# The second feed-forward product with its contraction split over two halves of the array

## The reference, cut to what matters

```
def conv_ffn(h, w_up, conv_w, conv_b, w_down):
    S = h.shape[1]
    u = h @ w_up                                   # 2048 -> 2 * 5632
    up = jnp.pad(u, ((0, 0), (CONV_W - 1, 0), (0, 0)))
    c = conv_b
    for i in range(CONV_W):
        c = c + up[:, i:i + S] * conv_w[i]
    gate, val = jnp.split(c, 2, axis=-1)
    return (jax.nn.gelu(gate, approximate=True) * val) @ w_down   # 5632 -> 2048
...
    x = x + rmsnorm(conv_ffn(h, w_up[l], conv_w[l], conv_b[l], w_down[l]), post_ffn_g[l])
```

## Time and profile before

| | us |
|---|---|
| median of 3 runs | 3087.95 (3086.61 to 3098.1) |
| span of the profiled execution | 3083.6 |
| PE busy in it | 2762.9 (90%) |
| DVE busy | 1585.5 (51%) |
| ACT busy | 1189.2 (39%) |
| first to last matmul start of the job "down" | 1272.5 to 1520.5 |

### The profile page before, as it was taken

The page is one execution under the profiler, slowest core; times in us unless marked ns, Lnnn a source line. Parts: engine busy times, 40 slices in busy tenths (PEclk is TensorE's granted clock), DMA queues, the critical chain, the costliest instruction groups (busy, mean ns, idle before and its releaser), DMA issues.

```text
span 3083.6 us, 33688 instructions
## 1 busy us (share of the span) xinstructions
PE 2762.9 (90%) x13763; PEld 2314.9 (75%) x13763; DVE 1585.5 (51%) x1634; ACT 1189.2 (39%) x1230; POOL 230.3 (7%) x234
## 2 busy tenths in 40 slices
PE   5999999996999999899799978679999598888986
PEld 4876888875887888788688867558888488787875
DVE  3445444644556556544444434565554366655635
ACT  3335333644455445433333454333443222222232
POOL 1002000000000000000000000000000232332210
PEclk9999999998999999999899989889999699989998
DMA  6554666653555555566555533445666401121042
GB/s 187 196 156 48 205 209 203 205 164 132 182 179 175 190 177 177 196 196 194 168 166 191 193 120 110 157 143 177 223 213 205 101 1 29 35 46 34 1 183 90
DMA packets 231320, 459.29 MB, mean 149 GB/s; under 512 B 9767, under 2 KB 29320, under 8 KB 228909
## 3 DMA queue, kind: packets, MB, share of 16 engines
q1 hardware_dynamic: 221584, 419.99, 42.6%
q0 software_dynamic: 8640, 35.36, 4.3%
q10 hardware_dynamic: 988, 2.41, 0.2%
HBM read 443.00 MB, written 14.71 MB: 148 GB/s over the span
## 4 chain that ended last, share of the span: by engine, by line
PE 43%; DVE 5%; ACT 3%; DMA 3%; POOL 3%; SPq 1%; issue 1%; DVEq 0%; ACTq 0%; POOLq 0%
PE bank L286 11%; PE bank L287 11%; PE bank L288 11%; PE bank L1626 2%; DMA d_lora_out<-in_od_a 2%; PE bank L1628 2%; PE bank L1616 2%; PE bank L1461 1%; DMA raw<-in_od_w_o 1%; SPq L1441 1%; PE bank L1584 1%; PE bank L1872 1%; PE bank L386 1%; DVE X L1310 1%; DVE d_step L1643 0%
## 5 line engine op out<-in xcount | busy, mean ns | idle before, releaser
L231 DVE TENSOR_TENSOR w_low<-raw,w_high 128x2048 fp32r<-128x2048 f32 (+1 forms) x384 | 875.8, 2281 | 1087.9 <-ACT w_high L225 1087.8
L225 ACT ACTIVATE w_high<-raw 128x2048 fp32r<-128x2048 f32 (+1 forms) x384 | 732.4, 1908 | 1232.1 <-PE bank L288 1208.3
L286 PE MATMUL bank<-w_high,b_h_high 128*128 128x512 f32 x704 | 278.0, 395 | 12.5 <-DVE w_low L231 10.0
L288 PE MATMUL bank<-w_high,b_h_low 128*128 128x512 f32 x704 | 274.8, 390 | 0.0
L287 PE MATMUL bank<-w_low,b_h_high 128*128 128x512 f32 x704 | 274.5, 390 | 0.0
L286 PE MATMUL bank<-w_high,a_h_high 128*128 128x512 f32 (+1 forms) x640 | 246.4, 385 | 2.1 <-DVE a_bias_rows L735 2.1
L288 PE MATMUL bank<-w_high,a_h_low 128*128 128x512 f32 (+1 forms) x640 | 246.3, 385 | 0.0
L287 PE MATMUL bank<-w_low,a_h_high 128*128 128x512 f32 (+1 forms) x640 | 246.1, 385 | 0.0
L286 PE MATMUL bank<-w_high,d_high 128*128 128x512 f32 x512 | 200.4, 391 | 8.1 <-DVE d_low L1946 8.1
L286 PE MATMUL bank<-w_high,c_x_high 128*128 128x512 f32 x512 | 199.9, 390 | 2.0 <-DVE c_x_low L409 2.0
L287 PE MATMUL bank<-w_low,c_x_high 128*128 128x512 f32 x512 | 199.9, 390 | 0.0
(11 more groups left out here) (365 smaller groups left out, 4548.5 us busy)
## 6 DMA issues: line engine op xcount, KB each, us to landing
raw<-in_w_up SPq DMA_DIRECT2D x88, 1024.0 KB, 5.0
raw<-in_w_in SPq DMA_DIRECT2D x76, 1024.0 KB, 5.1
raw<-in_ev_w_in SPq DMA_DIRECT2D x48, 1024.0 KB, 5.1
raw<-in_w_down SPq DMA_DIRECT2D x44, 1024.0 KB, 5.1
raw<-in_w_out SPq DMA_DIRECT2D x16, 1024.0 KB, 5.2
raw<-in_ev_w_out SPq DMA_DIRECT2D x16, 1024.0 KB, 5.2
raw<-in_od_w_r SPq DMA_DIRECT2D x16, 1024.0 KB, 5.1
raw<-in_od_w_k SPq DMA_DIRECT2D x16, 1024.0 KB, 5.5
```

Of the source, the lines that this page charges most:

```text
L225: act.activation(wh[slot % 2][:, :, 0:width], raw[slot][:, :, 0:width], ACT.Copy).then_inc(sem("w_high_made"), 1)
L231: vec.tensor_tensor(wl[slot % 2][:, :, 0:width], raw[slot][:, :, 0:width], wh[slot % 2][:, :, 0:width].bitcast(F32), ALU.subtract).then_in ...
L286: pe.matmul(b, xh, wh[slot][:, k, 0:width], start=(c == 0 and k == 0), stop=False)
L288: mm = pe.matmul(b, xl, wh[slot][:, k, 0:width], start=False, stop=(c == j.chunks - 1 and k == 3))
```

## The change

Each matmul of the job "down" is replaced by two. One takes rows 0 to 63 of both operands, the other rows 64 to 127; rows of the operands are rows of the array. The first half's sum is kept in bank t (0 or 1), the second half's in bank 2 + t. All four banks now belong to each panel, and at its end ACT copies banks 0 and 1 to `YB`, and DVE adds banks 2 and 3 to it. `acc_free` is incremented by DVE's second addition, and a panel waits for the one just before it (P + 2). The splits of the weights, the transfers and all other jobs are as they were.

```diff
+    def row_products(pe, j, p, g, P, ready=None):
+        width = j.weights(p)[3]
+        pe.wait_ge(sem("acc_free"), P + 2)
+        for c in range(j.chunks):
+            slot = (g + c) % 2
+            hi, lo, k0 = j.stationary(p, c)
+            pe.wait_ge(sem("w_low_made"), g + (c + 1))
+            for k in range(4):
+                if ready is not None:
+                    ready(c, k)
+                first, last = c == 0 and k == 0, c == j.chunks - 1 and k == 3
+                for t in range(2):
+                    for x, w, start, stop in ((hi, wh, first, False), (hi, wl, False, False), (lo, wh, False, last)):
+                        for half in range(2):
+                            r = slice(64 * half, 64 * half + 64)
+                            mm = pe.matmul(PS[2 * half + t][:, 0:width], x[r, k0 + k, 128 * t:128 * t + 128],
+                                           w[slot][r, k, 0:width], start=start, stop=stop)
+            mm.then_inc(sem("w_used"), 1)
+
+    def copy_first_rows(act, j, p, g_end, out):
+        width = j.weights(p)[3]
+        act.wait_ge(sem("w_used"), g_end)
+        act.activation(out(0), PS[0][:, 0:width], ACT.Copy)
+        act.activation(out(1), PS[1][:, 0:width], ACT.Copy).then_inc(sem("first_rows"), 1)
+
+    def add_last_rows(vec, j, p, out):
+        width = j.weights(p)[3]
+        vec.wait_ge(sem("first_rows"), p + 1)
+        vec.tensor_tensor(out(0), PS[2][:, 0:width], out(0), ALU.add)
+        vec.tensor_tensor(out(1), PS[3][:, 0:width], out(1), ALU.add).then_inc(sem("acc_free"), 1)
...
-        run_pe(pe, plan["down"], lambda c, k: pe.wait_ge(sem("ff_low_made"), c + 1) if k == 0 else None)
+        jd = plan["down"]
+        for p in range(jd.panels):
+            row_products(pe, jd, p, jd.g0 + p * jd.chunks, jd.p0 + p,
+                         (lambda c, k: pe.wait_ge(sem("ff_low_made"), c + 1) if k == 0 else None) if p == 0 else None)
...
-        run_act(act, jd, lambda p, t: YB[:, t, PANEL * p:PANEL * p + PANEL])
+        for p in range(jd.panels):
+            for c in range(p * jd.chunks, (p + 1) * jd.chunks):
+                splits(act, True, jd, c, 1)
+            copy_first_rows(act, jd, p, jd.g0 + (p + 1) * jd.chunks, lambda t: YB[:, t, PANEL * p:PANEL * p + PANEL])
...
-        run_vec(vec, plan["down"])
+        jd = plan["down"]
+        for p in range(jd.panels):
+            for c in range(p * jd.chunks, (p + 1) * jd.chunks):
+                splits(vec, False, jd, c, 1)
+            add_last_rows(vec, jd, p, lambda t: YB[:, t, PANEL * p:PANEL * p + PANEL])
```

## The result

The changed kernel takes 3118.55 us (median of 4 runs, 3116.28 to 3118.98). The kernel before, in the runs beside it, takes 3093.02 (3086.61 to 3101.97). The ratio is 1.0081 with a 95% interval of 1.0063 to 1.0099: 0.8% slower, 25.5 us. The forecast was 3115 us, +27.3 us and 0.88%.

The account below looks back on a forecast made before the run. PE was taken to set the pace in the job "down". Pairs 0, panel-end waits 17.6, clock 7.0 and job end 2.7 sum to 27.3 us, on 3087.95 giving 3115 us (0.88% slower); range 3097 to 3142.

Parts of the forecast that it names:

- A pair costs 227 ns: Matmuls of the job "down": two halves run side by side for what one full matmul cost; 1056 x 0 = 0 us.
- B: Matmul pairs: halves overlap but pay weight overhead one after the other, 240 ns a pair; 14.3 us more, 3129.5 us; chance 0.18.
- C: Matmul pairs: one half streams while the other changes weights, 213.5 ns a pair; -14.3 us, 3101 us; chance 0.14.
- D: Matmul pairs: fp32r halves are not run in parallel, 454 ns a pair; 239.7 us more, 3355 us; chance 0.13.
- The overhead of 13.5 ns: Each matmul of the job: the part of 227 ns beyond 213.5 ns of pure streaming, most likely the change of weights.
- the second of a pair starts 13 ns behind: Matmul pairs: second half starts 13 ns after the first, taken from the score matmuls, 0.01 to 0.02 us.
- The wait at the panel ends: Three panel ends: PE waits for DVE's additions behind its split, losing 5.9 us each, 17.6 us in all.
- The clock: After each panel-end wait PE works at the lower clock, 2.3 us lost each, 7.0 us in all; bounds nothing to 3 each.
- The end of the job: After the last matmul: ACT's sum of squares waits for DVE's additions, 2.7 us, all passed on.
- The start of the job: First panel's wait (P + 2) asks for a panel PE's transposes already wait for: nothing; the initial 5.5 us idle stays.

Follow-up runs that it names:

- eight banks: Changed kernel, but even panels use banks 0 to 3 and odd panels banks 4 to 7; ratio 1.0013 to the kernel before.
- quarters: Changed kernel, but in panels 2 to 4 each matmul becomes four on 32 rows, into all eight banks; 3133.16 us.
- blocks: Changed kernel, but per chunk all 24 matmuls of rows 0 to 63 come first, then all 24 of rows 64 to 127; 3631.15 us.
- one half: Changed kernel, but the matmuls on rows 64 to 127 run only in a panel's first and last groups; 3255.75 us.
- same rows: Changed kernel, but both matmuls of each pair use rows 0 to 63; 3665.36 us.
- full rows: Changed kernel, but matmuls on all 128 rows, even k to banks 0 and 1, odd k to banks 2 and 3; ratio 1.0078 to the kernel before.
- early end: Kernel before, but at the end of the job's last panel the copies, shared by ACT and DVE, come before the weight split; ratio 0.9990 to before.
- copies first: Changed kernel, but ACT's copies and DVE's additions of a panel stand before its last weight split; ratio 1.0027 to the kernel before.

## Why the prediction was right

**A pair costs 227 ns.** Right: two in 0.23 us, and under 1 ns of difference per pair with eight banks. The score matmuls of before had shown that rows of the array work in parallel; the open point, whether they do so at the full rate of fp32r, is settled, and quarters do it too. Rivals B (240 ns), C (213.5 ns) and D (in series) are gone. The overhead of 13.5 ns stays with one, two or four parts. That the second of a pair starts 13 ns behind was wrong as a general figure: together the two take 0.40 to 0.43 us, one 0.386, so it is some 10 to 44 ns, and it does not matter.

**The wait at the panel ends.** Right in place, order and size: 5.76 to 5.79 us against 5.9 forecast (17.3 in all instead of 17.6), released by DVE's second addition. The additions take 0.68 us each and overlap to 1.28.

**The clock.** Right in kind, a little small: 2.7 to 2.9 us a panel end instead of 2.3, 8.4 instead of 7.0 in all, with 13 or 14 slow distances instead of some 10. This term is the largest error of the sum, and what brings the trace from the forecast 27.3 to 28.7. I had taken the value from one earlier restart; the measured one lies inside the stated bounds (nothing to 3 us). Its idle time was as long, so how long the lower level lasts after the restart varies, and one row was too little for the value.

**The end of the job.** 2.55 us against 2.7.

**The start of the job** cost nothing, as said. The 25.5 us between the medians (interval 19 to 31) and the 28.7 us in the trace agree, or 27.0 with the 1.7 us that came back in the next job. That the last figure is so near to 27.3 is partly luck: the clock took 1.4 us more than forecast, and the clock of the next job, which the forecast did not speak of, gave 1.7 back. The absolute 3115 us is 3.6 too low because the forecast started from a median of 3087.95 us for before, and the runs beside the changed kernel gave 3093.02. The last 5 us of the difference between the two spans are, for the most part, the clock in the last round, which the forecast did not speak of either.

## What to carry to other kernels

Splitting a contraction that already fills the array's rows gives nothing: parts on different rows run side by side, even four of them, at the pace of one. What it takes is banks, and if these were the spare ones, each panel end becomes a wait whose length is whatever stands before the read-out in the queues of the reading engines. To judge such a change, follow the release of the bank through both queues and add the time at the lower clock, which here was 2.7 to 2.9 us for each wait of 5.8.

## What the runs showed of the hardware that was not expected

- Work on half of the array's rows mostly did not bring the clock back. After an idle time of 6 us PE was busy without a gap for 100 us and more on 64 rows at a time and stayed at 1.2 GHz (427 ns a matmul); pairs on all rows were back at 2.4 GHz after about 6 us. In the run with blocks an idle time of 2.1 us before the job was enough for the lower level in the whole job. The one exception is the 61 us in the run with one half. Half-row work that started at the upper level kept it (90 us in the run with the same rows). Which property of the work decides was not tried further.
- PE starts matmuls of another row part ahead of earlier listed ones, but with a short reach: the first of the next block started beside the fourth last of the 24 before it.
- An idle time of 2.5 us was once without effect on the clock and twice lowered it for a shorter time (loss of under 2 us). One of 2.1 us before the job lowered it in some traces (before, after, full rows, eight banks, blocks, early end) and not in others (copies first, one half, same rows, quarters). Those of 5.2 us and more in the job always lowered it, with a loss of 1.5 to 2.9 us where all rows were at work.
